# Rows of the normalised activations 2112 bytes apart instead of 2048, and the buffers behind them 512 bytes further on

## The reference

```python
for i in range(DEPTH):                     # DEPTH = 2, D_MODEL = 1024, SEQ = 256, D_FF = 2816
    x = x + 0.5 * swiglu(rms_norm(x, ffn1_norm[i]), ffn1_w_in[i], ffn1_w_out[i])
    hm = rms_norm(x, mix_norm[i])
    if i < N_A:                            # block 0
        x = x + retention(hm, ret_w_in[i], ret_w_out[i])
    else:                                  # block 1
        x = x + window_attention(hm, k_sh, v_sh, attn_w_q[j], q_norm[j], attn_sinks[j], attn_w_o[j])
    x = x + 0.5 * swiglu(rms_norm(x, ffn2_norm[i]), ffn2_w_in[i], ffn2_w_out[i])
    if i == N_A - 1:
        k_sh, v_sh = shared_kv(x, kv_norm, kv_w, k_norm)
```

## Time and profile before

| | us |
|---|---|
| median of 3 runs | 1026.74 (1025.99 to 1026.99) |
| the profiled execution, device time | 1026.68 |
| its span, first to last instruction | 1024.6 |
| PE busy | 1016.0 (99%) |
| DVE busy | 780.9 (76%) |
| ACT busy | 497.6 (49%) |
| POOL busy | 98.4 (10%) |

### The profile page before, as it was taken

One profiled execution on the slowest core, in us unless ns is written; L12 is line 12 of the kernel. 1 busy time (PEld: TensorE's weight loads), 2 busy tenths in 40 slices (PEclk: granted clock), 3 DMA queues, 4 the chain that ended last, 5 costly groups with the idle time before them and its releaser, 6 DMA issues.

```text
span 1024.6 us, 15884 instructions
## 1 busy us (share of the span) xinstructions
PE 1016.0 (99%) x5922; PEld 886.7 (87%) x5922; DVE 780.9 (76%) x874; ACT 497.6 (49%) x536; POOL 98.4 (10%) x91
## 2 busy tenths in 40 slices
PE   8999999999999999999999999999999999999998
PEld 7888888888888888888888888888887898888888
DVE  6987866788788678787777787788668877887743
ACT  7455434544444354454444454464457854554432
POOL 0000013101100152000013100000330031000000
PEclk9999999999999999999999999999999999999999
DMA  9765356653553444655455645534663245544461
GB/s 324 260 211 198 131 176 209 262 205 102 202 190 123 165 164 169 212 194 180 152 170 203 238 169 199 192 138 144 201 232 119 84 170 201 195 174 166 149 195 65
DMA packets 32292, 185.27 MB, mean 181 GB/s; under 512 B 3840, under 2 KB 6400, under 8 KB 16128
## 3 DMA queue, kind: packets, MB, share of 16 engines
q1 hardware_dynamic: 32112, 184.77, 51.1%
q10 hardware_dynamic: 144, 0.03, 0.0%
HBM read 183.73 MB, written 1.05 MB: 180 GB/s over the span
## 4 chain that ended last, share of the span: by engine, by line
PE 95%; ACT 1%; DVE 1%; DMA 1%; SPq 1%; POOL 0%; issue 0%; POOLq 0%; DVEq 0%; ACTq 0%
PE ps L1142 94%; DMA stage<-w_in_dram 1%; DVE w_lo L641 1%; PE ps L1421 0%; ACT w_hi L330 0%; SPq L288 0%; ACT s_own L520 0%; SPq L286 0%; ACT x_sq L614 0%; POOL y_sq L1128 0%; PE ps L1388 0%; DVE x_sq L1060 0%; DVE s_own L994 0%; ACT q_t L510 0%; DVE sm L975 0%
## 5 line engine op out<-in xcount | busy, mean ns | idle before, releaser
L1142 PE MATMUL ps<-h,w_hi 128*128 128x512 f32 x1664 | 584.1, 396 | 2.1 <-DVE h L680 1.4
L1142 PE MATMUL ps<-h,w_lo 128*128 128x256 f32 x1664 | 464.2, 279 | 0.0
L641 DVE TENSOR_TENSOR w_lo<-stage,w_hi 128x2048 fp32r<-128x2048 f32 (+1 forms) x190 | 396.9, 2098 | 29.6 <-ACT w_hi L330 29.3
L1142 PEld LDWEIGHTS ps<-h,w_hi 128*128 128x128 f32 x1664 | 312.1, 188 | 75.6 <-DVE w_lo L1076 1.0
L330 ACT ACTIVATE w_hi<-stage 128x2048 fp32r<-128x2048 f32 (+1 forms) x190 | 326.7, 1727 | 9.7 <-PE ps L1142 8.9
L1142 PEld LDWEIGHTS ps<-h,w_lo 128*128 128x128 f32 x1664 | 313.6, 188 | 0.3
L1142 PE MATMUL ps<-act_t,w_hi 128*128 128x512 f32 (+1 forms) x726 | 245.7, 387 | 0.0
L1142 PE MATMUL ps<-act_t,w_lo 128*128 128x256 f32 x704 | 196.3, 279 | 0.0
L1142 PEld LDWEIGHTS ps<-act_t,w_hi 128*128 128x128 f32 x726 | 134.7, 188 | 29.8
L362 ACT ACTIVATE tmp<-ps 128x1024 f32<-128x1024 f32 x44 | 45.2, 1026 | 192.8 <-PE ps L1142 192.8
L1142 PEld LDWEIGHTS ps<-act_t,w_lo 128*128 128x128 f32 x704 | 132.7, 188 | 0.0
(11 more groups left out here) (158 smaller groups left out, 739.1 us busy)
## 6 DMA issues: line engine op xcount, KB each, us to landing
stage<-w_in_dram SPq DMA_DIRECT2D x85, 1024.0 KB, 4.8
stage<-w_out_dram SPq DMA_DIRECT2D x64, 704.0 KB, 4.0
stage<-w_ret_dram SPq DMA_DIRECT2D x24, 1024.0 KB, 4.9
stage<-w_ret_out_dram SPq DMA_DIRECT2D x8, 1024.0 KB, 4.8
stage<-w_q_dram SPq DMA_DIRECT2D x4, 1024.0 KB, 4.9
stage<-w_o_dram SPq DMA_DIRECT2D x4, 1024.0 KB, 6.0
stage<-w_in_dram SPq DMA_DIRECT2D x8, 256.0 KB, 5.5
x<-x_t_dram SPq DMA_DIRECT2D x8, 128.0 KB, 5.9
```

What stands on the lines that cost most here:

```text
L641: nc.vector.tensor_tensor(w_lo[:, s, 0:n], stage[:, s, 0:n], w_hi[:, s, 0:n].bitcast(F32), ALU.subtract).then_inc(lo_ready, 1)
L1142: return nc.tensor.matmul(out_, w, x_, start=start, stop=stop)
```

## The change

The array `h` gets 16 more float32 columns per row, and a view leaves these out. Row d of `h` now begins 2112 * d bytes after the first, which has not moved. The eight rows take 512 bytes more (8 * 16 * 4), and all that lies behind counts from a `big` that is 512 bytes higher. The extra columns are neither written nor read. Every offset inside the later region stays, as does `s_two[1]`. The rows 1 to 7 of `h` thus begin 64, 128, 192, 256, 320, 384 and 448 bytes further past a multiple of 512 than before, and no other tile changes its place within 512 bytes.

The instructions of all five engines, with their shapes and waits, are the same in both kernels and stand in the same order. Only addresses differ. Line numbers above 61 are higher by one, and the trace calls the tile `h_rows`.

```diff
 WARM_UP = 9
 SLOTS = 4
+H_PAD = 16
 UNIT = 2048
 OUT_UNIT = FT // 2 * P
...
     x = at("x", [P, DT, T], F32, base + 98304)
-    h = at("h", [P, DT, 2 * T], F32R, base + 106496)
-    big = base + 122880
+    h = at("h_rows", [P, DT, 2 * T + H_PAD], F32R, base + 106496)[:, :, 0:2 * T]
+    big = base + 122880 + 4 * DT * H_PAD
     act_t = at("act_t", [P, FT, 2 * T], F32R, big)
     y_t = at("y_t", [P, YT, 2 * T], F32R, big)
```

## The result

| | before | after |
|---|---|---|
| median, us | 1026.37 (1024.2 to 1026.99, 6 runs) | 1034.02 (1033.76 to 1034.88, 6 runs) |
| ratio | | 1.008, 95% interval 1.007 to 1.0091 |
| profiled execution: device time, span | 1026.68, 1024.6 | 1034.88, 1032.8 |

The changed kernel is slower by 0.8%, about 7.7 us. The forecast was no change, 1026.7 us, with a range up to 1032.2, so the time lies outside it.

A forecast was written before the change was run, and what follows sets the result against it. The prediction took PE's distance from matmul to matmul to bound the kernel. Every term of the change was put at 0, so the forecast stayed at 1026.7 us, no change (0.66), with a range of 1021.5 to 1032.2 us.

The forecast's parts named there:

- What bounds the kernel: Whole kernel: PE busy 1016.0 of 1024.6 us, so time is the matmuls times their distance, plus less than 9 us.
- the price of 0 for instructions: All engines and queues: no instruction is added, removed or moved, so this term is 0.
- the writes of `h`: ACT's and DVE's writes of `h`: each one row, contiguous as before and mostly hidden behind pairs; taken as 0.
- the buffers 512 bytes further on: Buffers behind `h`: they keep their place within 512 bytes, only distance to weights and `stage` changes; taken as 0.
- PE's reads of `h` ... I take 0: 1664 pairs and 288 `token_block` matmuls reading `h`: moved rows change nothing, 0, between 9.7 us more and 38.8 us off.
- The bound above: PE's reads of `h`: at most every pair on a moved row goes from fast to slow distance, 9.7 us more.
- So the rhythm doesn't follow what is read: Pairs on `h` and `act_t`: both appear in fast and slow stretches, 346.7 or 353.3 ns, so the operand doesn't decide.
- The fixed rest of 13 ns: Every matmul on PE: 13 ns beyond one cycle a column, whatever its length and whichever operands.
- the bound below, the collision: Seven moved rows of `h`: the equal place of operands costs something the new spacing ends, up to 38.8 us off; chance 0.04.
- a row begins badly: Rows 1, 3, 5 and 7 of `h`: reads starting 64 bytes off take longer, 5.5 us more, 1032.2; chance 0.08.
- the rhythm falls another way: Long PE stretches: altered start switches rhythm, faster to 1022.5 to 1023.4 us (0.12) or slower up to 1030.2 (0.09).
- no stretch of this length flips between executions: Long stretches of pairs: runs lie within 1.0 us, so none changes rhythm; used against the rhythm turning slower.

The follow-up runs named there:

- the first experiment: Kernel before, rows of `h` still 2048 bytes apart and `h` in its place, only the buffers behind it 512 bytes further on: 1026.15 us, ratio 1.0001.
- the gap: Kernel before with 64 bytes put between `w_hi` and `w_lo`, so `w_lo` and every tile behind it begin 64 bytes later: 1010.96 us, ratio 0.9857.
- PE alone: Kernels without the model's computation, PE running pairs from fixed tiles at varied places, other engines at rest: 340.0 ns a pair with row and `w_lo` at 64.
- the table: Kernel without the model's computation, PE running 64 segments, row and `w_lo` each at 0 to 448 bytes in steps of 64: lowest cells at 64 or 320.

## Why the prediction was wrong, point by point

- **What bounds the kernel** was right: the distance from matmul to matmul, and nothing else moved. So were the price of 0 for instructions, for the writes of `h` (583 and 504 ns against 581 and 505) and for the buffers 512 bytes further on, which the first experiment shows alone.
- **"PE's reads of `h` ... I take 0"** is the step that failed. The runs showed +4.2 ns a pair on three feed-forwards' rows (346.7 to 350.9) and -2.4 in feed-forward 2 (353.3 to 350.9), +3.3 us in sum, and another 0.8 us for `token_block`. The bound above, 9.7 us, held it. A second term, for `act_t` behind these rows, was also put at 0 and measured +3.3 us. With 0.8 us of smaller ones that is the 8.2 us.
- The reason given for 0 was that no address had shown an effect. All operands had the same place within 512 bytes, so the trace had no power to show one. The prediction said that 64 bytes were new, and weighed them as if the steps of 512 were evidence. "So the rhythm doesn't follow what is read" was an inference from `h` and `act_t` at equal places.
- **The fixed rest of 13 ns** was taken for a cost of the matmul itself, since it was the same everywhere. At 340.0 ns a pair it is 10 ns each, so part of it belongs to the places. Of the bound below, the collision, some 15 us could be had in the whole kernel, but by the gap and not by spacing the rows of `h`. The Trainium skill, page "TensorE: Matmul & The Clock Gate", section "Step-by-step: what each phase is for", says that loading the next weights takes no read bandwidth from the running matmul. With PE alone, moving `w_lo` by 64 bytes with the row kept at 64 changes the pace from 353.3 to 340.0 ns. So the place of the weights does set a time. No run here shows whether read bandwidth is the reason.
- **The rival "a row begins badly"** named the place and the sign, with 0.08. Its price of 5.5 us was for odd rows alone, and 9.7 us for all seven moved. Rows at 128 and 384 bytes cost as well, 4.4 ns with PE alone, and the one at 256 doesn't. Its sign, a pattern with the row of `h`, is there; `act_t` as before, its other sign, is not.
- **The rival "the rhythm falls another way"** was right that short matmuls can set it (their order alone: 2.2 us on feed-forward 2's rows). It put the cause in a wait or a first read. With PE alone, rows with steps of 64 bytes leave it in the slow rhythm. That `act_t` inherits it so in the full kernel, +3.3 us, fits and is argued, since no run there turned the three projections back. Its sign of a faster feed-forward 2, 657 matmuls in 114 us, left out the two that the count adds: 346.7 ns a pair would give 660.
- **The range** held each rival alone and not both, though both came together: 1026.7 + 5.5 + 3.5 = 1035.7 by the prediction's own terms. It had left out seven slow rows, 1036.4, too. And "no stretch of this length flips between executions" doesn't follow from three runs. Six runs of the kernel before go from 1024.2 to 1026.99, and two executions took different rhythms on retention's output projection. That a stretch of over 100 us flips is likely by the times. No trace shows it.

What stays open: why a short matmul turns the rhythm from some states only, why `act_t` is fast behind slow rows of `h` at 64 and slow behind rows 2112 bytes apart, and what in memory or in the array makes a place good. That loading weights and reading a row hinder each other is argued from the table, where both places count, and not shown.

## What to carry to other kernels

Where PE is busy all the time, work out the distance between matmuls and hold it against their columns; what is above may hang on where the operands begin within 256 bytes, and a gap of 64 bytes between two tiles was worth 1.4% here, and 1.8% together with another order of a few short matmuls. Measure a table of places with PE alone before padding anything: 64 bytes more on each row of `h` cost 0.8%, and 64 bytes ahead of `h` alone 1.0%. And where all operands share one alignment, their equal pace says nothing on other alignments.

## What the runs showed of the hardware that I had not expected

- The pace of a pair of 512 and 256 columns with new weights each goes from 340.0 to 353.3 ns with the places of row and `w_lo` in steps of 64 bytes, at a full granted clock and with the other engines at rest. One single case with the row at 16 bytes took 360.0 at first and 346.7 behind a short matmul.
- At many places PE has two stable rhythms, 346.7 and 353.3 ns or 340.0 and 350.0. It kept one for over 100 us at a time. Short matmuls or another place could turn it, and two executions of one stream took different ones.
- The pattern repeats with 256 bytes: so does the table with PE alone, and a gap of 320 gives 1007.45 us where a gap of 64 gives 1007.6.
